# A chunked recurrence: two heads as diagonal blocks of one 128x128 matrix, and outputs with channels on partitions

## What is computed

```python
def step(S, inp):
    r_t, kk_t, v_t, w_t, b_t, k_t = inp
    sa = jnp.einsum('bhij,bhj->bhi', S, kk_t)
    S = S * w_t[:, :, None, :] - sa[..., None] * b_t[:, :, None, :] + v_t[..., None] * k_t[:, :, None, :]
    return S, jnp.einsum('bhij,bhj->bhi', S, r_t)
```

## Time and profile before

| | |
|---|---|
| median of 3 runs | 4764.63 us (4757.97 to 4789.08) |
| the profiled execution, its own time | 4777.09 us |
| its span | 4775.2 us |
| mean granted TensorE clock | 0.817 |
| TensorE, weight load, VectorE, ScalarE, GpSimd busy | 79%, 57%, 48%, 14%, 29% |
| the recurrence, first to last TensorE record | 648.6 to 1268.4 us |

### The profile page before, as it was taken

The page is one execution under the profiler, slowest core; times in us unless marked ns, Lnnn a source line. Parts: engine busy times, 40 slices in busy tenths (PEclk is TensorE's granted clock), DMA queues, the critical chain, the costliest instruction groups (busy, mean ns, idle before and its releaser), DMA issues. The chain is left out here.

```text
span 4775.2 us, 42350 instructions
## 1 busy us (share of the span) xinstructions
PE 3792.6 (79%) x15936; PEld 2730.4 (57%) x15936; DVE 2280.3 (48%) x4406; ACT 683.9 (14%) x1541; POOL 1396.2 (29%) x1178
## 2 busy tenths in 40 slices
PE   7889978998864665666666789877887788989899
PEld 3446557877531222324244578655776567877687
DVE  2441153333247777576576676777764321023201
ACT  2111021111111111111112110121101211012100
POOL 1620011111005666464753455554550000000000
PEclk9886955555587888888886799887998889998899
DMA  6310300000018888787984699986993013421243
GB/s 188 96 53 19 88 2 1 1 1 1 23 51 279 314 299 306 261 307 273 376 309 152 229 361 394 348 281 229 377 394 114 32 53 126 156 98 53 77 153 106
DMA packets 439153, 833.41 MB, mean 175 GB/s; under 512 B 46435, under 2 KB 281374, under 8 KB 438942
## 3 DMA queue, kind: packets, MB, share of 16 engines
q0 software_dynamic: 147456, 536.94, 30.8%
q1 hardware_dynamic: 291494, 293.76, 19.2%
HBM read 828.44 MB, written 2.17 MB: 174 GB/s over the span
## 5 line engine op out<-in xcount | busy, mean ns | idle before, releaser
L2347 PE MATMUL banks<-arena 128*128 128x256 f32 (+1 forms) x4992 | 1166.2, 394 | 95.3 <-DVE arena L2417 43.4
L2347 PEld LDWEIGHTS banks<-arena 128*128 128x128 f32 (+1 forms) x4992 | 980.5, 198 | 273.8 <-issue 65.9
L1936 POOL DMA_INDIRECT arena<-in_peer_v,arena x512 | 631.6, 1234 | 796.0 <-DVE arena L2045 484.1
L2056 DVE CUSTOM_DVE_ANT_0 arena<-arena 128x1024 f32<-128x1024 f32 x512 | 628.0, 1227 | 225.3 <-DMA arena<-in_peer_u,arena 208.8
L2003 PE MATMUL banks<-arena 128*128 128x512 f32 x768 | 436.0, 707 | 310.4 <-ACT arena L2021 193.1
L1936 POOL DMA_INDIRECT arena<-in_peer_u,arena x512 | 550.9, 1076 | 406.4 <-issue 368.9
L2003 PEld LDWEIGHTS banks<-arena 128*128 128x128 f32 x768 | 160.3, 223 | 557.4 <-issue 329.6
L2045 DVE SCALAR_TENSOR_TENSOR arena<-arena 128x1024 f32<-128x1024 f32 x316 | 406.2, 1285 | 28.3 <-DMA arena<-in_peer_v,arena 18.0
L617 PE MATMUL banks<-arena 128*128 128x512 f32 (+1 forms) x768 | 309.3, 561 | 1.8 <-DVEq L283 1.8
L3113 PE MATMUL banks<-arena 128*128 128x256 f32 x1408 | 310.4, 378 | 0.0
L3155 DVE TENSOR_TENSOR arena<-banks,arena 128x512 f32<-128x512 f32 x44 | 30.4, 692 | 540.6 <-PE banks L2347 540.5
(11 more groups left out here) (336 smaller groups left out, 4405.0 us busy)
## 6 DMA issues: line engine op xcount, KB each, us to landing
arena<-in_l_w_gate SPq DMA_DIRECT2D x44, 1024.0 KB, 6.7
arena<-in_l_w_up SPq DMA_DIRECT2D x44, 1024.0 KB, 9.6
arena<-in_l_w_down SPq DMA_DIRECT2D x44, 1024.0 KB, 5.1
arena<-in_ada_w SPq DMA_DIRECT2D x24, 1024.0 KB, 8.0
arena<-in_l_w_qkv SPq DMA_DIRECT2D x24, 1024.0 KB, 5.3
arena<-in_w_in SPq DMA_DIRECT2D x36, 512.0 KB, 4.0
...
```

Of the source, the lines that this page charges most:

```text
L1936: p.e.indirect_dma_start(e.ring[slot], None, tables[table], bass.IndirectOffsetOnAxis(ap=e.IDX[h][:, t, j:j + 1], axis=0)).then_inc(*p.up( ...
L2056: p.e.tensor_tensor_reduce(out=e.prod, in0=e.ring[slot], in1=e.H2[:, t, :], scale=1.0, scalar=0.0, op0=ALU.mult, op1=ALU.add, accum_out=e. ...
L2347: ins = p.e.matmul(out, left(c), right(c), start=c == 0, stop=c == c_n - 1, skip_group_check=True)
```

## The change

In the new chunk work the two heads of a slot are the two 64x64 blocks on the diagonal of one 128x128 matrix. AB, BB, KB, VB, NT and M2 are stored as such matrices with zeros beside the diagonal, written once (`off_blocks`: 12 memsets on VectorE for one set of buffers, 12 on GpSimd for the other), and each writer touches the diagonal blocks alone. N, X, A, Y, the inverse, RH, U and the sum are four matmuls 128x128 by 128 columns for each chunk, in place of eight 64x64 by 64. M1 and M2 are four each with 64 (context) or 128 columns (latent), where eight were. Tb's start is no longer masked by VectorE but transposed by TensorE (T0) and copied by ScalarE. The wait for T of the level before stands ahead of A and no longer ahead of X. The keys are copied into AB by ScalarE, two ACTIVATEs, between the keys on VectorE and the first matmul. The output of a latent chunk is 12 matmuls with 64 columns whose result has channels on partitions (`outputs_pe`); its four transposes and the copy before them are gone. The mask in the state's scaling is gone. The new functions `turned` and `products` are in the diff; `windows` gives both directions' 64 tokens as one operand, so that pairs of operations become one. Of removed lines the diff shows none: they are in the functions printed above.

```diff
...
 class Chunk:
+    def __init__(self, A, B, ring):
+        self.E1, self.KR = B.take(2, 2, 64), B.take(4, 2, 64)
         at = A.at
+        self.AB, self.BB, self.KB, self.VB, self.NT, self.M2 = (A.take(4, P) for _ in range(6))
+        self.blocks = A.t[:, at:A.at].rearrange("p (m s a n) -> p m s a n", m=6, s=4, a=2)
+        self.Bt, self.Kt, self.Vt, self.Ta, self.Tb, self.No, self.NTo = (A.take(4, P) for _ in range(7))
+        self.M1R, self.M2R = A.take(4, 64), A.take(4, 64)
+        at = A.at
+        self.E2, self.E3 = A.take(2, 2, 64), A.take(2, 2, 64)
+        A.at = at
+        self.Xs = A.take(4, P)
         self.ring = ring
...
 def rwkv_memory(k, rw, A):
+    rw.RH, rw.U = spare1.take(4, P), spare1.take(4, P)
...
+    rw.idb = k.ident[:, None, :].to_broadcast([P, 4, P])
...
+    rw.sets = [Chunk(slots, A, (0, 1, 2)), Chunk(A, A, (3, 4, 5))]
...
+def off_blocks(k, p, j, signal):
+    for a in range(2):
+        rows = slice(64 * a, 64 * a + 64)
+        for m in range(6):
+            p.in_order()
+            p.e.memset(k.rw.sets[j].blocks[rows, m, :, 1 - a, :], 0.0).then_inc(*p.up(signal))
...
 def chunk_pe(k, p, c):
+    p.wait_ge(S.chunk_copied, (c, "inputs"))
+    for step, (name, left, right, w) in enumerate((
+            ("N", B.AB, lambda s: B.BB[:, s, :], P),
+            ("M1", B.BB, lambda s: B.KR[:, s, 0:nk, :], 64 * nk),
+            ("M2", B.KB, lambda s: B.KR[:, s, 0:nk, :], 64 * nk))):
+        bank = chunk_bank(k, B, c, step)
+        p.claim(chunk_place(B, c, step), S.chunk_kept, (c, name))
         for s in range(4):
+            ins = p.e.matmul(bank[:, s * P:s * P + w], left[:, s, :], right(s), start=True, stop=True, skip_group_check=True)
         ins.then_inc(*p.up(S.chunk_filled, (c, name)))
         yield
...
+    def turned(step, name, src, signal):
+        bank = chunk_bank(k, B, c, step)
+        p.claim(chunk_place(B, c, step), signal, (c, name))
+        for s in range(4):
+            ins = p.e.transpose(bank[:, s * P:s * P + P], src[:, s, :], k.ident)
+        ins.then_inc(*p.up(S.chunk_filled, (c, name)))
+    def products(step, name, left, right, signal):
+        bank = chunk_bank(k, B, c, step)
+        p.claim(chunk_place(B, c, step), signal, (c, name))
+        for s in range(4):
+            ins = p.e.matmul(bank[:, s * P:s * P + P], left[:, s, :], right[:, s, :], start=True, stop=True, skip_group_check=True)
+        ins.then_inc(*p.up(S.chunk_filled, (c, name)))
+    turned(3, "Bt", B.BB, S.chunk_copied)
+    yield
+    p.wait_ge(S.chunk_kept, (c, "Ta"))
+    turned(4, "T0", B.Ta, S.chunk_copied)
+    yield
+    turned(5, "Kt", B.KB, S.chunk_copied)
+    yield
+    p.wait_ge(S.chunk_prepared, (c, "values"))
+    turned(6, "Vt", B.VB, S.chunk_copied)
+    yield
     for l in range(1, 5):
         p.wait_ge(S.chunk_prepared, (c, "NTo", l))
+        products(4 + 3 * l, f"X{l}", B.NTo, B.Ta, S.chunk_copied)
+        yield
+        p.wait_ge(S.chunk_copied, (c, f"X{l}"))
+        p.wait_ge(S.chunk_copied if l % 2 else S.chunk_kept, (c, f"T{l - 1}"))
+        products(5 + 3 * l, f"A{l}", B.Tb, B.Xs, S.chunk_kept)
+        yield
+        p.wait_ge(S.chunk_kept, (c, f"A{l}"))
+        turned(6 + 3 * l, f"T{l}", B.Ta, S.chunk_kept if l % 2 else S.chunk_copied)
+        yield
+    p.wait_ge(S.chunk_copied, (c, "T4"))
+    products(19, "Y", B.No, B.Tb, S.chunk_copied)
     yield
     p.wait_ge(S.chunk_copied, (c, "Y"))
+    products(20, "inverse", B.Ta, B.Xs, S.chunk_kept)
     yield
...
 def chunk_act(k, p, c):
         p.wait_ge(S.state_ready, c - 2)
+    p.e.activation(B.E2, windows(rw.Ls, c), ACT.Exp, scale=-1.0).then_inc(*p.up(S.decay_exp, (c, 2)))
+    p.wait_ge(S.decay_diff, c)
+    p.e.activation(B.E3, B.E3, ACT.Exp).then_inc(*p.up(S.decay_exp, (c, 3)))
+    if c >= 4:
+        p.e.activation(B.E1, windows(rw.Ls, c), ACT.Exp).then_inc(*p.up(S.decay_exp, (c, 1)))
+    p.wait_ge(S.chunk_kept, (c, "keys"))
+    for a, h in enumerate(HEAD):
...
+    def copied(step, name, dst):
         p.wait_ge(S.chunk_filled, (c, name))
+        p.e.activation(flat(dst), chunk_bank(k, B, c, step), ACT.Copy).then_inc(*p.up(S.chunk_copied, (c, name)))
+    for _ in range(3):
+        yield
+    for step, name, dst in ((3, "Bt", B.Bt), (4, "T0", B.Tb), (5, "Kt", B.Kt), (6, "Vt", B.Vt)):
+        copied(step, name, dst)
         yield
     for l in range(1, 5):
...
 def chunk_dve(k, p, c):
     if c >= 2:
         p.wait_ge(S.state_filled, (c - 2, "last"))
     p.in_order()
+    p.e.tensor_tensor(B.E3, windows(rw.Ls, c), windows(rw.LW, c), ALU.subtract).then_inc(*p.up(S.decay_diff, c))
+    p.wait_ge(S.decay_exp, (c, 2))
+    for h in HEAD:
+        p.e.tensor_tensor(B.BB[h, :, h].rearrange("p (d g) n -> p d g n", d=2), windows(rw.Bd, c, h), B.E2[h], ALU.mult).then_inc(
+            *p.up(S.vector_step))
+    p.wait_ge(S.decay_exp, (c, 3))
     for d in range(2):
         p.e.tensor_tensor(B.KR[:, SL[d], 0, :], window(rw.KKn, c, d), B.E3[:, d], ALU.mult).then_inc(
+            *(p.up(S.chunk_kept, (c, "keys")) if d else p.up(S.vector_step)))
+    if latent:
+        p.wait_ge(S.decay_exp, (c, 1))
+        for d in range(2):
+            p.e.tensor_tensor(B.KR[:, SL[d], 1, :], window(rw.Z[:, 0:2, :], c, d), B.E1[:, d], ALU.mult).then_inc(
+                *(p.up(S.chunk_kept, (c, "inputs")) if d else p.up(S.vector_step)))
+    else:
+        p.in_order()
+        p.e.drain().then_inc(*p.up(S.chunk_kept, (c, "inputs")))
     yield
+    bank = chunk_bank(k, B, c, 0)
+    p.wait_ge(S.chunk_filled, (c, "N"))
+    for name, dst, last in (("m_first", B.Ta, None), ("m_last", B.No, (c, "N"))):
+        m = rw.mk[name].rearrange("p (d n) -> p d n", n=64)[:, :, None, :].to_broadcast([P, 2, 4, 64])
+        p.e.tensor_tensor(by_direction(flat(dst)), by_direction(bank), m, ALU.mult).then_inc(
+            *(p.up(S.chunk_kept, last) if last else p.up(S.vector_step)))
+    p.in_order()
+    p.e.tensor_tensor(B.Ta, B.Ta, rw.idb, ALU.add).then_inc(*p.up(S.chunk_kept, (c, "Ta")))
+    yield
+    for step, name, mask, dst, rows in ((1, "M1", "m_bk", B.NT, B.M1R), (2, "M2", "m_kk", B.M2, B.M2R)):
+        src = chunk_bank(k, B, c, step).rearrange("p (d g n) -> p d g n", d=2, g=2)
+        m = rw.mk[mask].rearrange("p (d n) -> p d n", d=2)[:, :, None, :].to_broadcast([P, 2, 2, P])
+        p.wait_ge(S.chunk_filled, (c, name))
+        for a, h in enumerate(HEAD):
+            p.e.tensor_tensor(dst[h, :, h].rearrange("p (d g) n -> p d g n", d=2), src[h, :, :, 0:64], m[h, :, :, 0:64],
+                              ALU.mult).then_inc(*(p.up(S.chunk_kept, (c, name) if not latent else (c, name, "left")) if a else
+                                                   p.up(S.vector_step)))
+        if latent:
+            p.e.tensor_tensor(rows.rearrange("p (d g) n -> p d g n", d=2), src[:, :, :, 64:P], m[:, :, :, 64:P],
+                              ALU.mult).then_inc(*p.up(S.chunk_kept, (c, name)))
+        yield
+    for _ in range(4):
+        yield
+    for l in range(1, 5):
+        yield
+        p.wait_ge(S.chunk_filled, (c, f"A{l}"))
         p.in_order()
+        p.e.tensor_tensor(flat(B.Ta), chunk_bank(k, B, c, 5 + 3 * l), flat(B.Ta), ALU.add).then_inc(*p.up(S.chunk_kept, (c, f"A{l}")))
         yield
         if l % 2:
+            p.wait_ge(S.chunk_filled, (c, f"T{l}"))
+            p.e.tensor_copy(flat(B.Tb), chunk_bank(k, B, c, 6 + 3 * l)).then_inc(*p.up(S.chunk_kept, (c, f"T{l}")))
         yield
     yield
     p.wait_ge(S.chunk_filled, (c, "inverse"))
+    p.e.tensor_tensor(flat(B.Tb), chunk_bank(k, B, c, 20), flat(B.Tb), ALU.add).then_inc(*p.up(S.chunk_kept, (c, "inverse")))
     yield
...
 def chunk_pool(k, p, c):
+    B, latent = rw.sets[c % 2], c >= 4
+    def off_diagonal(l):
+        lv = rw.levels[:, l - 1, :][:, None, :].to_broadcast([P, 8, 64])
+        p.in_order()
+        p.e.tensor_tensor(flat(B.NTo).rearrange("p (x n) -> p x n", n=64), flat(B.NT).rearrange("p (x n) -> p x n", n=64), lv,
+                          ALU.mult).then_inc(*p.up(S.chunk_prepared, (c, "NTo", l)))
     if c >= 2:
         p.wait_ge(S.state_filled, (c - 2, "last"))
+    p.wait_ge(S.decay_exp, (c, 2))
+    for h in HEAD:
+        p.in_order()
+        p.e.tensor_tensor(B.KB[h, :, h].rearrange("p (d g) n -> p d g n", d=2), windows(rw.Kd, c, h), B.E2[h], ALU.mult).then_inc(
+            *(p.up(S.chunk_prepared, (c, "inputs")) if h.start else p.up(S.pool_scaled)))
     for d in range(2):
+        for h in HEAD:
+            p.in_order()
+            p.e.tensor_copy(B.VB[h, SL[d], h], window(rw.V, c, d)[h]).then_inc(
+                *(p.up(S.chunk_prepared, (c, "values")) if d and h.start else p.up(S.pool_scaled)))
+    yield
+    yield
+    p.wait_ge(S.chunk_kept, (c, "M1", "left") if latent else (c, "M1"))
+    off_diagonal(1)
+    for _ in range(6):
         yield
     for l in range(1, 5):
...
 def state_pe(k, p, c, between):
     p.wait_ge(S.state_ready, c - 1)
     p.wait_ge(S.chunk_kept, (c, "inverse"))
```

(39 more changed lines are left out.)

239 lines of the change are left out of this document (50 added, 189 removed).

## The result

The changed kernel takes **4523.91 us** (median of 4 runs, 4510.65 to 4547.44) where the kernel before took 4763.19 (4 runs beside it): ratio 0.9491, 95% interval 0.9459 to 0.9522. The forecast was 4530, range 4490 to 4640. The profiled execution is the slowest of the four, 4547.44 us, with a span of 4545.6.

The account below looks back on a forecast made before the run. TensorE at 1.2 GHz was taken to bound the serial recurrence stage. Four latent pairs save 189 us, two context pairs 60, memsets add 4: 245 less, 4777.1 - 245 = 4532, given as 4530, range 4490 to 4640.

Parts of the forecast that it names:

- latent: state work: RH, U, sum, next state and outputs of a latent pair's two chunks: 19.0 us for 39.3.
- The bound and the serial stage: Recurrence: bound by TensorE at 1.2 GHz, serial between barriers; TensorE busy 100.0 of 110 us per latent pair.
- The levels at 1.00: Four levels of each pair: TensorE at 2.4 GHz, 5.3 us a level, 21.2 for 35.5.
- The 0.2 for GpSimd beside VectorE: Levels: GpSimd's mask overlaps VectorE's add, which costs up to 1.14 instead of 0.68; a level 5.3, not 5.1 us.
- First phase, latent: Latent pair, first N to X: 14.5 us for 25.6; 72 dense records, the clock rising after 5 us, VectorE later.
- the wait ahead of Kt: Latent first phase: TensorE waits for VectorE before Kt, as the ring of three banks holds Kt for M2's masking.
- Rival 2: State work: clock rises for the levels but falls here; +70 us, 4602; chance 0.15.
- Rival 4: Levels bound by ScalarE, VectorE and GpSimd at 6 us or more, first phases by VectorE; +42, 4572; chance 0.07.
- Rivals 1 and 3: Stage: 1, clock stays 1.2 GHz, 4716, chance 0.09; 3, also records cost 0.053 more, 4838, chance 0.04.
- the cause given for the clock: Whole stage: the matmuls' shape sets the clock; 64x64 stay at 0.50, 128x128 run at 1.00.
- bubble of some 3 us before X: End of the latent first phase: a bubble of some 3 us ahead of X, counted as gone with the change.
- rival 1: Stage: clock stays at 1.2 GHz; latent pair 95.8 us, its state work 32.3; 61 us less, 4716; chance 0.09.

Follow-up runs that it names:

- kernels 1, 2, 5, 6: Changed kernel with 64x64 products: grouped by head (1: 4500.46 us), in turn (2: 4520.36); T's transposes 64x64 too, in turn (5: 4486.14), grouped (6: 4520.5).
- kernel 6: Changed kernel with all products and T transposes of the levels as 64x64 blocks, grouped by head: 4520.5 us.
- kernel 9: Kernel before, with 8 and 24 dummy 128x128 transposes in the wait ahead of level 1, levels untouched: 4739.58 us.
- kernel 7: Kernel before, with four dummy 128x128 transposes ahead of the wait of each T step of the levels: 4838.62 us.
- kernel 11: Kernel before, with dummy transposes both in the wait ahead of level 1 and ahead of each T step of the levels: 4666.42 us.

## Why the prediction was right, and where its reason was not

By its own terms:

| term, us | forecast | measured |
|---|---|---|
| latent: gap before N | 3.9 | 3.7 |
| latent: first N to X | 14.5 | 14.1 to 14.5 |
| four levels | 21.2 | 20.3 |
| Y and inverse | 4.0 | 3.8 |
| latent: state work | 19.0 | 19.4, once 20.8 |
| latent pair | 62.6 | 61.3, 61.5, 63.1 |
| context: first N to X | 17.4 | 18.2, 17.8 |
| context pair | 62.2 | 62.3, 64.7 |
| stage, memsets left out | -249 | -249 |

- *The bound and the serial stage*: right. All of the stage's loss is the program's loss.
- *The levels at 1.00*: right, and the steps within a level too (the first T starts 3.69 us after X, given as 3.80). The 0.2 for GpSimd beside VectorE was wrong: the add stays at 0.69 (group of VectorE in the stage, below), so a level is 5.08, not 5.3. That is 0.9 us a pair.

```profile
L1522 DVE TENSOR_TENSOR arena<-banks,arena 128x512 f32<-128x512 f32 x48 | 33.2, 691 | 83.0 <-PE banks L1399 83.0
```

- *First phase, latent*: 14.1 for 14.5, but by another path. The prediction has TensorE done 9.8 us after the first N and VectorE set the rest. By its own terms (2.9, then 5 us at the low clock and 48.5 records of 0.108) TensorE is done at 13.1. In the trace the second chunk's N starts 3.59 us after the first, and from there TensorE is busy 10.35 of the 10.47 us to X; the wait ahead of Kt that I had named as a sign is not in this pair and is 0.20 us in the one before it.

```profile
912.09:922.56 10.47, 10.35 (x72) 10.11 (x73) 8.04 (x18) 3.20 (x7) 2.47 (x3) 0.79 0.01 2
```

- *64 columns are no cheaper than 128 under 128x128 weights*: right, 0.213 and 0.112 us from start to start for both.
- *The copy into AB*: given as 0.8, measured 0.41 us each; TensorE waits 3.45 us in all, until the second has ended.

```profile
L1444 ACT ACTIVATE arena<-arena 64x256 f32<-64x256 f32 x22 | 9.1, 414 | 14.2 <-DVE arena L1484 9.1 <-DVEq L1493 4.8
```

- *Memsets*: given as +4. VectorE's 12 take 3.3 us and lie between barriers; the stretch about them is 5.
- *Other stages*: given as 0 within 10 us or so. Between the two profiled executions they moved by 19.5 us, and by 37 among all traces, so that the total came within 7 us of the forecast is in part luck. The stage is what the prediction got right.
- *Rival 2* had a grain: the clock did fall in the state work of the second and the third pair (0.83 and 0.92 on average), and those two pairs are 64.7 and 63.1 us long, where their like are 62.3 and 61.4. It cost some 4 us, not 70. *Rival 4* (levels of 6 us) did not come: VectorE is idle 83 us waiting for TensorE in the levels. *Rivals 1 and 3* are out, the clock being 0.88 in the stage.

**The step that failed is the cause given for the clock.** I took dense 64x64 matmuls at 0.50 and 128x128 ones at 1.00 for a property of the shape, and worked out from it that the levels would run at 1.00. They did, but the reason does not give it, so that this condition of the whole sum was met by luck. The runs show something else in its place:

1. 64x64 products run at 1.00 in the changed layout (kernels 1, 2, 5, 6) and, for one to three levels, in the old one (kernel 9).
2. What the clock does depends on what it was. It came up in the kernel before as well, at the end of each pair's first phase, and was dropped at a wait of 2.5 us, the "bubble of some 3 us before X" that I had priced at its length alone. A stream that keeps a clock once it is up need not raise it: kernels 7 and 11 run one and the same at 0.50 and at 1.00.
3. What holds it is not how busy TensorE is by the profile (94% held it in kernel 6, 96% lost it in kernel 9). The levels of kernel 6 held it, with blocks in two corners of the array, and those of kernel 9 did not, with blocks in one; 128x128 records among the latter held it (kernel 11). Whether the corners, the form of T or the number of records makes the difference between 6 and 9 is open.

So the change did three things that I had put down as one. It took the wait ahead of level 1 away (X follows the transposes at once). It has the clock up before the levels: in three of the four latent pairs it rises about 8 us after the first N, among the products, and in the context pairs after 16 to 17 us, among the transposes. And its levels are of a kind that holds it. That each of them is needed is argued from kernels 7, 9 and 11, in the old layout; no kernel takes one of them out of the changed one.

Where the 249 us of the stage lie, added up over the six pairs from the same timelines, and what kernel 11 gains in the same parts over the kernel before:

| part | before, us | after | saved | kernel 11 saves |
|---|---|---|---|---|
| first N to X | 128.2 | 92.6 | 35.6 | -0.7 |
| levels | 224.7 | 122.0 | 102.7 | 59.1 |
| Y and inverse | 42.1 | 23.0 | 19.2 | 18.9 |
| state work and outputs | 208.3 | 111.9 | 96.4 | 18.8 |
| gaps between pairs | 16.2 | 21.0 | -4.8 | 0 |

The wait ahead of level 1, 2 us a pair, is in the row of the levels. What of the rest is the clock's can only be estimated. In the levels, Y and the inverse it is about 104 of the 122: a level with the old code takes 5.33 us at 1.00 for 8.87 (kernel 9), Y and the inverse 3.88 for 7.02 (kernel 11), and 6 x (4 x 3.54 + 3.14) = 104. In the state work it was not tried by itself. By rival 1's working (32.3 for 39.3 at the low clock) it is about 13 of the 20 us of a latent pair, and 7 are the form's; in kernel 11 the clock stays up for the first 4 to 7 us of the old state work, and these do what took 1.5 to 1.6 times as long before, which comes to about the same. In a latent first phase it is about 4 of the 9.5 us: 18.2 by rival 1's working if the clock stayed low, 14.1 measured. The rest there is fewer matmuls and masks, as priced.

The Trainium skill ("TensorE: Matmul & The Clock Gate", Part 1) says that a gap in the work lets the clock fall. The waits of kernels before and 7 agree with that, though at 2.51 us they are shorter than the gaps it warns of. The same part of the Trainium skill has sustained busyness bring the clock back. The 18 us at 0.50 in the kernel before and the 22 us of kernel 7 disagree.
